# The first fixed expert's rows found from its own ranks ahead of the row table, the rest of the routing moved under its products, and no barrier

## The reference, cut to what matters

```python
def hier_moe(h, wg, bg, we, be, w1, w3, w2):
    ...
    p_grp = jax.nn.softmax((hf @ wg + bg).astype(jnp.float32), axis=-1)
    pg_top, grp = lax.top_k(p_grp, 1)
    le = (hf @ we + be).astype(jnp.float32).reshape(T, MOE_GROUPS, EXPERTS_PER_GROUP)
    p_in = jax.nn.softmax(le[jnp.arange(T), grp], axis=-1)
    pe_top, e_in = lax.top_k(p_in, TOP_K_IN_GROUP)
    gate = pg_top * pe_top / jnp.sum(pe_top, axis=-1, keepdims=True)
    eidx = grp[:, None] * EXPERTS_PER_GROUP + e_in
    y = grouped_expert_ffn(hf, eidx, gate.astype(h.dtype), w1, w3, w2)
...
    def run_block(args):
        toks, gts, ei = args
        xb = hf[toks]
        hb = jax.nn.silu(xb @ w1[ei]) * (xb @ w3[ei])
        return (hb @ w2[ei]) * gts[:, None]
```

## Time and profile before

| | us |
|---|---|
| median of 3 runs | 1486.21 (1485.47 to 1486.59) |
| the profiled execution, its own time | 1481.07 |
| its span (first to last instruction) | 1479.2 |
| PE busy in the span | 1338.3 (90%) |
| DVE busy | 626.8 (42%) |
| ACT busy | 398.8 (27%) |
| POOL busy | 120.7 (8%) |
| bytes moved | 306.29 MB, mean 207 GB/s |
| mean granted clock of PE | 0.966 of 2.4 GHz |

### The profile page before, as it was taken

One profiled execution on the slowest core, in us unless ns is written; L12 is line 12 of the kernel. 1 busy time (PEld: TensorE's weight loads), 2 busy tenths in 40 slices (PEclk: granted clock), 3 DMA queues, 4 the chain that ended last, 5 costly groups with the idle time before them and its releaser, 6 DMA issues.

```text
span 1479.2 us, 16991 instructions
## 1 busy us (share of the span) xinstructions
PE 1338.3 (90%) x6325; PEld 674.4 (46%) x6325; DVE 626.8 (42%) x1377; ACT 398.8 (27%) x888; POOL 120.7 (8%) x148
## 2 busy tenths in 40 slices
PE   5899999999997798999999962999999999989964
PEld 3644444464564444544555541454444444434421
DVE  3526347520234676666556556233232222222317
ACT  4243311112576555555423220000000000000004
POOL 0000000000000700000010000011110111111110
PEclk9999999999998999999999975999999999999997
DMA  9812235330002500000064485899999999999969
GB/s 339 181 43 68 104 136 203 116 115 0 1 1 84 36 1 1 1 0 1 1 242 158 155 317 202 312 397 395 395 407 391 406 402 394 399 411 395 409 265 400
DMA packets 90527, 306.29 MB, mean 207 GB/s; under 512 B 28317, under 2 KB 32573, under 8 KB 82121
## 3 DMA queue, kind: packets, MB, share of 16 engines
q1 hardware_dynamic: 83160, 288.34, 52.4%
q0 software_dynamic: 6736, 16.81, 3.2%
q10 hardware_dynamic: 544, 0.02, 0.0%
HBM read 282.54 MB, written 27.82 MB: 210 GB/s over the span
## 4 chain that ended last, share of the span: by engine, by line
PE 38%; DMA 9%; SPq 5%; DVE 4%; issue 2%; ACT 1%; PEldq 0%; PEld 0%; DVEq 0%; ACTq 0%; POOLq 0%
DMA arena<-expert_w 7%; PE ps L1710 7%; PE ps L1699 7%; PE ps L1628 7%; PE ps L1749 6%; SPq L711 4%; PE ps L1507 2%; PE ps L1526 2%; PE ps L1546 2%; PE ps L1689 2%; PE ps L1580 1%; DMA arena<-d_y 1%; ACT arena L1143 1%; SPq L803 1%; PE ps L1564 0%
## 5 line engine op out<-in xcount | busy, mean ns | idle before, releaser
L1357 PE MATMUL ps<-arena 128*128 128x512 f32 x512 | 222.0, 593 | 0.0
L1710 PE MATMUL ps<-arena 128*32 128x256 f32 (+1 forms) x1408 | 187.8, 481 | 13.0 <-DMA arena<-expert_w 11.1
L1749 PE MATMUL ps<-arena 128*32 128x256 f32 (+2 forms) x832 | 152.7, 498 | 3.4 <-issue 1.8
L1357 PEld LDWEIGHTS ps<-arena 128*128 128x128 f32 x512 | 96.6, 190 | 117.8 <-issue 117.7
L1368 PE MATMUL ps<-arena 128*128 128x512 f32 (+1 forms) x384 | 144.6, 535 | 1.4 <-DVE arena L1853 1.4
L1710 PEld LDWEIGHTS ps<-arena 128*32 128x32 f32 (+1 forms) x1408 | 70.9, 122 | 115.6 <-issue 98.4
L1699 PE MATMUL ps<-arena 128*128 128x512 f32 x256 | 114.8, 606 | 2.8 <-DVE arena L2348 2.8
L1143 ACT ACTIVATE arena<-arena 128x640 f32<-128x640 f32 (+7 forms) x128 | 92.8, 726 | 61.7 <-DVE arena L2067 61.7
L1368 PEld LDWEIGHTS ps<-arena 128*128 128x128 f32 x384 | 72.8, 192 | 66.3 <-issue 57.3
L2067 DVE CUSTOM_DVE_ANT_0 arena<-ps,arena 128x640 f32<-128x640 f32 (+7 forms) x128 | 84.5, 705 | 39.8 <-PE ps L1507 37.6
L1526 PE MATMUL ps<-arena 128*128 128x128 f32 x528 | 82.0, 288 | 21.2 <-ACT arena L1143 13.2
(11 more groups left out here) (366 smaller groups left out, 1364.4 us busy)
## 6 DMA issues: line engine op xcount, KB each, us to landing
arena<-expert_w SPq DMA_DIRECT2D x96, 2048.0 KB, 33.9
arena<-ada_w SPq DMA_DIRECT2D x12, 2048.0 KB, 9.2
arena<-x SPq DMA_DIRECT2D x16, 512.0 KB, 5.1
arena<-w_in SPq DMA_DIRECT2D x4, 2048.0 KB, 10.7
d_xn<-arena SPq DMA_DIRECT2D x8, 1024.0 KB, 4.2
arena<-d_y SPq DMA_DIRECT2D x16, 512.0 KB, 10.4
arena<-w_out SPq DMA_DIRECT2D x2, 2048.0 KB, 10.7
d_x<-arena SPq DMA_DIRECT2D x8, 512.0 KB, 2.9
```

The costliest lines, as they stand in the source:

```text
L1357: last = nc.tensor.matmul(b, w(k), hT[:, k, 512 * c:512 * c + 512], start=(k == 0), stop=(k == KT - 1))
L1710: last = nc.tensor.matmul(ps[width * j:width * j + width, 2 if width == 64 else 3, 0:span], xgT[s][:, k, lo:lo + width], w_up[slots[n]][:, ...
L1749: last = nc.tensor.matmul(dst, hid_T[s][:, at_:at_ + width], w_down[slot][:, k, span * j:span * j + span], start=(k == 0), stop=(k == 3))
```

## The change

1. DVE no longer takes the whole table before the first gather. Behind `hots` it takes for expert 0 alone: a lane number for each token (`lane_0`, its rank in the expert, or a number out of range), a one-hot matrix `lane_hot0` (half the size), and a token number with tile and position (`tok_pair`). PE multiplies eight pairs of tiles into two columns (job "table0"), and DVE writes column 0 of `row_tok`. POOL gathers step 0 from that.
2. `expert_at` is made as soon as `place` is known, and SP waits for it (`expert_known`) in place of the barrier and `table_ready`.
3. `f_turned(0)` stands on DVE ahead of the operations on `far`, `slot`, `dest`, `tok_hot` and `lane_hot`. PE multiplies the whole table (`whole_table`) between the first and the second eight products of `f_up(0)`. The four operations on the gates (L2257 to L2260) go behind `lane_hot`.
4. The barrier "E" is gone from all engines. POOL waits for "table0" to be read before gather 0, and for "table" before gathers 1 to 3.
5. ACT takes the silu of step 0 ahead of the ten small transfers; DVE scales their result behind `hidden_turned(0)` instead of ahead of step 0.
6. The three routing banks are 6, 5 and 7 instead of turn banks. Six constant tables are made by POOL after the last `x2_done`, in another place of memory, and the routing's scratch is laid out anew so that `xg` and `xgT` of step 0 don't overlap what is still in use.

```diff
@@ SP @@
-            sp.wait_ge(stage_end["E"], 4)
-            sp.wait_ge(table_ready, 1)
+            sp.wait_ge(expert_known, 1)
             for v in range(NS - 1, len(LOADS)):
@@ POOL @@
+            pool.wait_ge(x2_done, NT)
+            nc.gpsimd.iota(tile_no, [[NT, 2], [1, NT]], base=-4 * NT, channel_multiplier=0,
+                           allow_small_or_imprecise_dtypes=True).then_inc(late_const, 1)
...
             for s in range(2):
                 pool.wait_ge(xn_stored[s], 16 * NT // 2)
-            end_stage(pool, "E")
...
-            for q in range(4):
+            was_read(pool, "table0")
+            gather_rows(0)
+            was_read(pool, "table")
+            for q in range(1, 4):
                 gather_rows(q)
@@ ACT @@
-            end_stage(act, "E")
...
+            gated(0, 0, STEP_ROWS[0])
             act.wait_ge(row_f_ready, 1)
...
-            for q in range(NQ):
+            for q in range(1, NQ):
                 gated(q, q % 2, STEP_ROWS[q])
@@ PE @@
+            b = claim(pe, "table0")
+            for t in range(NT):
+                if t % 4 == 0:
+                    pe.wait_ge(early_hot, t // 4 + 1)
+                last = nc.tensor.matmul(b[:, 0:2], lane_hot0[:, t, :], tok_pair[:, t, :], start=(t == 0), stop=(t == NT - 1))
             last_of(last)
-            end_stage(pe, "E")
+            def whole_table():
+                b = claim(pe, "table")
+                pe.wait_ge(toks_hot, 2)
+                for n in range(2 * NT):
+                    if n % 4 == 0:
+                        pe.wait_ge(slots_hot, n // 4 + 1)
...
@@ f_up, a block of 128 rows @@
                         last.then_inc((up_half, up_done)[n], 1)
+                        if n == 0 and between:
+                            between()
@@ DVE @@
-            dve.wait_ge(exps_done, 2)
-            link(V.tensor_reduce(sg_, dg, AX.X, ALU.add))
-            link(V.scalar_tensor_tensor(sg_, e2, 1.0, sg_, ALU.add, ALU.mult))
-            link(V.reciprocal(gates2[:, 0, :], sg_))
-            link(V.tensor_tensor(gates2[:, 1, :], gates2[:, 0, :], e2, ALU.mult))
+            dve.wait_ge(hots_ready, 1)
+            dve.wait_ge(late_const, 3)
+            link(V.tensor_scalar(not_hot, hots[:, :, e0], -512.0, 512.0, ALU.mult, ALU.add))
+            link(V.scalar_tensor_tensor(tok_pair[:, :, 0], h1_[:, :, e0], float(NT), tile_no[:, 0:NT], ALU.mult, ALU.add))
+            link(V.tensor_copy(tok_pair[:, :, 1], pos_id.broadcast_to([P, NT])))
...
+            link(V.tensor_tensor_scan(run_0, ones32[:, 0:NT], b[:, 256:512].rearrange("p (t e) -> p t e", e=NE)[:, :, e0], 0.0,
+                                      ALU.mult, ALU.add))
+            link(V.tensor_tensor(lane_0, b[:, 0:256].rearrange("p (t e) -> p t e", e=NE)[:, :, e0], run_0, ALU.add))
+            link(V.tensor_tensor(lane_0, lane_0, not_hot, ALU.add))
+            for n in range(0, NT, 4):
+                V.tensor_tensor(lane_hot0[:, n:n + 4, :], iota128.unsqueeze(1).broadcast_to([P, 4, P]),
+                                lane_0[:, n:n + 4].unsqueeze(2).broadcast_to([P, 4, P]), ALU.is_equal).then_inc(early_hot, 1)
...
+            b = ready(dve, "table0")
+            link(V.tensor_scalar(tile_part[:, 0:1], b[:, 0:1], float(P), float(4 * S), ALU.mult, ALU.add))
+            read(V.tensor_tensor(row_tok[:, 0:1], b[:, 1:2], tile_part[:, 0:1], ALU.add), "table0")
...
+            V.tensor_copy(expert_at, own_sum).then_inc(expert_known, 1)
...
+            dve.wait_ge(mod_hop, 96)
+            f_turned(0, 0, STEP_ROWS[0], True)
             link(V.tensor_tensor(far, rank, row(cap), ALU.is_ge))
...
-            end_stage(dve, "E")
...
                 hidden_turned(q, q % 2, STEP_ROWS[q], q < 2)
+                if q == 0:
+                    dve.wait_ge(parts_in, 160)
...
```

More of the change, by code:

```diff
@@ L138 @@
 TURN_BANKS = (1, 2, 3)
+ROUTE_BANK = {"rank": 6, "table0": 5, "table": 7}
 P_BANK = {6: 6, 7: 6, 5: 5, 4: 5, 3: 7}
@@ L434, in build @@
         own_sum = route(1)
-        ov_cmp = route(NOV, NE)
         tabf = route(32)
@@ L438, in build @@
         lane_f, blk_f = route(2, NT), route(2, NT)
+        not_hot, run_0, lane_0 = (route(NT) for _ in range(3))
+        tok_pair = route(NT).bitcast(BF16).rearrange("p (t a) -> p t a", a=2)
         w_up = [view(at_, KT, FF) for at_ in SLOT]
@@ L1690, in f_turn, with f_up @@
                 last.then_inc(xg_turned, 1)
-            def f_up(q, s, rows, slots, loaded):
+            def f_up(q, s, rows, slots, loaded, between=None):
                 pe.wait_ge(xgT_ready, q + 1)
@@ L2254, in _, with f_turned @@
             V.tensor_tensor(hots, h0, h1_, ALU.add).then_inc(hots_ready, 1)
-            dve.wait_ge(exps_done, 2)
-            link(V.tensor_reduce(sg_, dg, AX.X, ALU.add))
-            link(V.scalar_tensor_tensor(sg_, e2, 1.0, sg_, ALU.add, ALU.mult))
-            link(V.reciprocal(gates2[:, 0, :], sg_))
-            link(V.tensor_tensor(gates2[:, 1, :], gates2[:, 0, :], e2, ALU.mult))
+            def f_turned(q, s, rows, first=False):
+                dve.wait_ge(xg_turned, q + 1)
+                if not first:
+                    dve.wait_ge(up_done, q - 1)
+                for k in range(KT):
+                    last = V.tensor_scalar(xgT[s][:, k, 0:rows], turned_at(k, rows), scale_f[:, k:k + 1], shift_f[:, k:k + 1], ALU.mult, ALU.add)
+                last.then_inc(xgT_ready, 1)
+            e0 = PINNED[ORDER[0]]
+            dve.wait_ge(hots_ready, 1)
[3 more added lines that the diff above has]
+            link(V.tensor_copy(tok_pair[:, :, 1], pos_id.broadcast_to([P, NT])))
             V.memset(ones32, 1.0)
@@ L2275, in _ @@
             link(V.tensor_reduce(place, pair_cmp, AX.X, ALU.add))
+            dve.wait_ge(late_const, 6)
+            link(V.scalar_tensor_tensor(own, place, pos_id, iota32, ALU.is_equal, ALU.mult))
+            link(V.tensor_reduce(own_sum, own, AX.X, ALU.add))
+            V.tensor_copy(expert_at, own_sum).then_inc(expert_known, 1)
             V.tensor_scalar(top, place, 3.0, None, ALU.is_equal)
@@ L2339, in _ @@
             V.tensor_copy(block_tab, tabf[0:1, :]).then_inc(table_ready, 1)
-            def f_turned(q, s, rows, first=False):
-                dve.wait_ge(xg_turned, q + 1)
-                if not first:
-                    dve.wait_ge(up_done, q - 1)
-                for k in range(KT):
-                    last = V.tensor_scalar(xgT[s][:, k, 0:rows], turned_at(k, rows), scale_f[:, k:k + 1], shift_f[:, k:k + 1], ALU.mult, ALU.add)
-                last.then_inc(xgT_ready, 1)
             def hidden(q, s, rows):
```

105 lines of the change are left out of this document (55 added, 50 removed).

## The result

| | us |
|---|---|
| changed kernel, median of 5 runs | 1476.04 (1474.47 to 1476.95) |
| before, median of 5 runs | 1485.47 (1482.0 to 1486.59) |
| ratio, 95% interval | 0.9937 [0.9921, 0.9953] |
| the profiled execution, its time and span | 1474.47, 1472.6 |

The change makes the kernel 9.4 us faster (0.63%, between 7.0 and 11.7 by the interval); 11.0 were forecast and the time lies in the stated range. In the profiled execution the routing starts later than in the one of before: `hots` ends at 888.70 instead of 886.81. Over all profiles of this case that end lies between 886.8 and 890.7, also for kernels with the same program up to there, so I count from the end of `hots` where executions are compared.

The account below looks back on a forecast made before the run. PE and DMA were taken as nearly in balance from 940 us on, so only an earlier start helps. Terms -12.9, +1.2 and +0.7 make -11.0 us, from 1486.2 to 1475.2; range 1470.5 to 1480.5 (chance 0.81).

Parts of the forecast that it names:

- The sum: Whole kernel: -12.9 us at step 0, +1.2 for the table on PE, +0.7 for step 1's gather, making -11.0.
- What bounds the stage: From 940 us on, DMA and PE nearly in balance; PE waits for weights 11.1 us in six waits.
- To the gather: Routing up to the first gather's issue: at 892.5 instead of 908.26 us, 15.8 us earlier.
- The landing: First gather's landing beside weight loads: 8 us taken instead of 5.2, bounds 5.2 and 9.5.
- the first-come order: First gather standing behind all loads in flight: it would land at about 898 + 5 = 903 us.
- Step 0: First expert step: products begin at 905.4 us (bounds 902.5 and 907), table adds 1.2 on PE, end at 923.4.
- Step 1: Second expert step: waits for the table's gather; products begin at 926.3 to 928.3, 11.7 to 9.7 us earlier, 11 taken.
- the rival at 1482: PE's clock stays at half through step 0's products, 6.9 us more; within the less-gain case, 1478 to 1485, chance 0.17.
- step 2's at 938 to 940: Sign in the profile: the third expert step's products begin at 938 to 940 us, before at 949.82.
- Load 9: Weight load issued at 896.6 instead of 912.64 us; said to give nothing of itself, as step 1 waits for load 10.
- The small columns: Ten transfers behind step 0, landing at about 931 us, 3 us of slack; rival: landing later makes it slower, chance 0.06.
- The stage behind: Everything after the first steps: same slot distances, bytes and clock, so it moves by the same 11 us.

Follow-up runs that it names:

- delay_start: The changed kernel plus seven linked memsets of 128x1024 on VectorE behind the sum of one-hots, ahead of expert 0's ranks; 1482.84 us, ratio 0.9984.
- gather0_from_table: The changed kernel without its own rank, one-hots and products for expert 0, so the first gather waits for the whole table; 1483.88 us, ratio 0.9994.
- late_load9: The changed kernel, but SyncE waits for the overflow table too before load 9, as before the change; 1483.17 us, ratio 0.9993.
- change_again: The changed kernel itself, unaltered, timed once more; 1476.67 us, ratio 0.9944 to the kernel before.
- busy_2_1: The changed kernel plus three unused PE products, two behind step 0's products, one behind the turn of its hidden values; 1474.40 us, repeated 1473.48.
- columns_ahead: The changed kernel with the scaling of the small columns back ahead of step 0's hidden values on VectorE; 1479.84 us, ratio 0.9966.
- moved_operations_alone: The changed kernel with the far and slot operations ahead of step 0's scaling and the gates behind row_tok, table products unmoved; 1475.92 us, ratio 0.9940.
- table_in_first_half: The changed kernel with the table multiplied behind step 0's sixth product instead of the eighth, and far, slot and gate operations moved; 1472.52 us, ratio 0.9913.

## Why the prediction was right

**The sum.** It said -11.0 and -9.4 was measured, by an interval that holds both. The mechanism is shown: the time behind `hots` is carried to the end (delay_start), it comes from the early gather, and neither the barrier nor load 9 does it alone (gather0_from_table). That the early gather does not do it alone either, but needs load 9, the prediction did not have (late_load9).

**What bounds the stage.** "11.1 us in six waits" left out a seventh, of 1.6 us; 12.7 of 500 us is still little, and nothing hangs on it.

**To the gather.** Forecast 5.7 us behind `hots` (892.5 - 886.81), measured 5.6 (894.30 - 888.70).

**The landing.** I took 8 us with bounds 5.2 and 9.5. From issue to turn it is 7.0 in the change, 7.6 in change_again, 8.6 in busy_2_1, and 5.2 where the loads had landed already (delay_start). I had the loads ahead of it landed at about 898; that was the middle of two landing times, and the last of them landed at 899.7 before (883.67 + 16.0) and at 900.7 in the change (885.71 + 15.0). The gather landed at 901.3, 0.6 us behind that load and not the 5 us behind that the first-come order gives. This agrees with the Trainium skill's "DMA: Bandwidth & Descriptors" (Queues, rings and completion order), by which a DMA engine takes turns between its queues: the gather moves beside the loads, and takes 1.8 us longer than without them.

**Step 0.** Products at 18.6 behind `hots` forecast, 17.4 measured. The first half took 8.55 us instead of 9.92, since the clock rose 2.8 us into it and not 5.6 as before (0.53 over 908 to 909 us and 1.00 behind it; before, 0.56 over 923 to 924); in change_again it is 9.57 (905.17 to 914.74). The table on PE took 1.29, forecast 1.2. The end of step 0's products was forecast 36.6 us behind `hots` and came at 34.0: 1.2 us from the start and 1.4 from the clock, neither of which the sum had.

**Step 1, the term that was mis-sized.** The bounds for its start, 39.5 to 41.5 behind `hots`, rest on the late gather: 38.6 measured, 0.9 us below them, with 1.59 us of wait for that gather. What I did not have is the price behind the wait. "Nothing up to the end depends on another clock than these steps" failed at once: the clock fell and step 1's products took 2.7 us more. I had looked for a slow clock in step 0's second half (the rival at 1482), where PE has no pause. The two errors, 2.6 us better to the end of step 0 and 2.7 worse at step 1, nearly cancel in this profile: step 2's products were forecast 51.3 to 53.3 us behind `hots` and came at 53.1, 9.9 us won for the 11.0 of the sum. That this came so near is in part luck. Counted from the beginning of the span the sign "step 2's at 938 to 940" was missed, 941.84, since `hots` ended 1.9 us later.

**Load 9.** "That gives nothing of itself" is right as measured, but the sentence hid that the gain needs it: with loads 9 and 10 held up, some 8 us are lost.

**The small columns.** Forecast to land at about 931, DVE went on at 930.28, and step 2 was not touched, so this rival did not come true; columns_ahead shows what the move avoided. I had read the same section of the Trainium skill, that a semaphore's increment lands only behind the DMA engine's earlier writes, as if the columns had to wait for all of load 11. That load was issued at 922.89 and took 9.6 us, to 932.5; the columns, issued until 923.9, counted 2.2 us earlier. So they did not wait for the whole of a load issued ahead of the last of them; my reading was wrong, and the measurement decides. Which of load 11's writes stood ahead of theirs on each DMA engine no row here shows.

**The stage behind.** I costed its change at nothing. From step 2's first product to the end of the span it is 529.4 us before and 530.8 in the change (1472.6 - 941.84), and over all profiles of this case between 529 and 533. The two lowest are those of the two kernels without the early gather, 529.4 (before) and 529.0 (gather0_from_table); the other ten lie between 530.7 and 532.7. So between one and four microseconds seem to be given back there. No run shows by what, and I put this term at nothing.

## What to carry to other kernels

Where a stage is saturated in both engine and transfers, ask when it starts: what its first step alone needs can be worked out ahead of the general answer, and the rest put under that step's products. Then look at the second step, since it waits for all that the first skipped: here its rows, its weights and the small columns each had to move too, and undoing one cost 3 to 8 us. Place the hidden work at the earliest point at which its inputs are ready and not at the next natural seam; here two products earlier were worth 4 us.

## What the runs showed of the hardware that I had not expected

A short added wait can cost more than itself on PE. With a pause of 1.6 to 2.0 us and one of 1.35 us close behind it, and only two short turns between, the clock fell from 2.4 to 1.2 GHz in each of the four profiles with that pair (the change, change_again, moved_operations_alone, delay_start), and the next 64 products took 5.1 to 6.4 us. With 1.35 us alone, in the kernel before, or 1.53 us in table_in_first_half, it held and they took 3.66. In the change the fall came as the second pause had just begun, in the three others within it, and no run has the longer pause without the 1.35; so whether it takes both is not shown. Three products whose results nobody reads, put into the pauses, kept the clock up in both profiles and made the kernel 2.3 us faster.
